# 8 of the 24 modulation units of the first attention layer move from TensorE to row products on VectorE, and the other 16 stand in a row behind units 31 to 46 of the hybrid block

## The reference, cut to what matters

```python
# first block: three branches from one wide product, gated and summed, then a feed forward
(hg_q, hg_f, hg_i, hg_g, ml_qk, ml_v, ml_if, ml_o, mb_z, mb_xbc, mb_dt, gate_pre) = split(rmsnorm(x) @ w_in)
x = x + (gates[0] * (y_hg @ w_br_hg) + gates[1] * (y_ml @ w_br_ml) + gates[2] * (y_mb @ w_br_mb)) @ w_out
u_g, u_v = split(causal_dwconv(rmsnorm(x) @ w_up))
x = x + (silu(u_g) * u_v) @ w_down
# two attention layers i = 0, 1
sh1, sc1, g1, sh2, sc2, g2       = split(silu(c)     @ w_ada[i] + b_ada[i], 6)    # w_ada[i] is 1024 x 6144
csh1, csc1, cg1, csh2, csc2, cg2 = split(silu(c_ctx) @ w_ada[i] + b_ada[i], 6)
h, hc = rms_norm(x) * (1 + sc1) + sh1, rms_norm(ctx) * (1 + csc1) + csh1
x = x + g1 * (mixed(h, hc) @ w_out[i])
x = x + g2 * conv_ffn(rms_norm(x) * (1 + sc2) + sh2)        # and the same for ctx in layer 0
```

## Time and profile before

| | |
|---|---|
| median of 3 runs | 1656.63 us (1656.02 to 1659.84) |
| span of the profiled execution | 1654.1 us |
| its own time | 1655.9 us |
| TensorE / VectorE / ScalarE / GpSimd busy | 97% / 74% / 53% / 11% |
| granted clock, mean | 0.995 |

### The profile page before, as it was taken

One profiled execution on the slowest core, in us unless ns is written; L12 is line 12 of the kernel. 1 busy time (PEld: TensorE's weight loads), 2 busy tenths in 40 slices (PEclk: granted clock), 3 DMA queues, 4 the chain that ended last, 5 costly groups with the idle time before them and its releaser, 6 DMA issues.

```text
span 1654.1 us, 34573 instructions
## 1 busy us (share of the span) xinstructions
PE 1596.3 (97%) x14802; PEld 1448.0 (88%) x14802; DVE 1215.8 (74%) x2069; ACT 881.4 (53%) x1344; POOL 189.4 (11%) x120
## 2 busy tenths in 40 slices
PE   8999999999999999999988999999999998799999
PEld 7999888898999999998867888888887897699999
DVE  4375499687877886588866788876888779568864
ACT  5435645548546665456775444323433456666653
POOL 4303540000000110100000011101110000041100
PEclk9999999999999999999999999999999999999999
DMA  7655555464455554531202243463435333045554
GB/s 280 249 215 227 195 219 183 169 230 179 145 187 179 184 191 158 182 109 54 76 2 74 107 153 128 146 232 142 155 136 207 110 103 103 3 157 200 202 167 143
DMA packets 41129, 259.67 MB, mean 157 GB/s; under 512 B 4368, under 2 KB 7696, under 8 KB 14480
## 3 DMA queue, kind: packets, MB, share of 16 engines
q1 hardware_dynamic: 40976, 257.46, 43.6%
HBM read 256.39 MB, written 1.05 MB: 156 GB/s over the span
## 4 chain that ended last, share of the span: by engine, by line
PE 68%; DVE 23%; ACT 4%; issue 2%; DMA 2%; DVEq 0%; SPq 0%; ACTq 0%
PE acc_psum L209 20%; PE acc_psum L210 19%; PE acc_psum L211 19%; DVE w_low_sb L174 5%; DVE mod_products L336 3%; DVE u_filtered L2116 2%; DVE ring_sb L336 2%; PE acc_psum L218 2%; DMA ring_sb<-in_w_up 1%; ACT w_high_sb L162 1%; PE acc_psum L2609 1%; DVE norm_rt_sb L1848 1%; PE acc_psum L272 1%; ACT norm_rt_sb L2869 1%; PE acc_psum L2638 1%
## 5 line engine op out<-in xcount | busy, mean ns | idle before, releaser
L209 PE MATMUL acc_psum<-h_high_sb,w_high_sb 128*128 128x256 f32 (+1 forms) x2176 | 655.8, 301 | 5.1 <-DVE h_low_sb L502 1.9
L210 PE MATMUL acc_psum<-h_low_sb,w_high_sb 128*128 128x256 f32 (+1 forms) x2176 | 647.9, 298 | 0.0
L211 PE MATMUL acc_psum<-h_high_sb,w_low_sb 128*128 128x256 f32 (+1 forms) x2176 | 647.9, 298 | 0.0
L162 ACT ACTIVATE w_high_sb<-ring_sb 128x1024 fp32r<-128x1024 f32 (+2 forms) x412 | 387.0, 989 | 359.3 <-PE acc_psum L211 212.5
L174 DVE TENSOR_TENSOR w_low_sb<-ring_sb,w_high_sb 128x1024 fp32r<-128x1024 f32 (+1 forms) x362 | 395.7, 1135 | 103.4 <-ACT w_high_sb L162 93.8
L209 PEld LDWEIGHTS acc_psum<-h_high_sb,w_high_sb 128*128 128x128 f32 x2176 | 411.1, 189 | 32.4 <-issue 12.7
L210 PEld LDWEIGHTS acc_psum<-h_low_sb,w_high_sb 128*128 128x128 f32 x2176 | 409.0, 188 | 15.5 <-issue 0.5
L211 PEld LDWEIGHTS acc_psum<-h_high_sb,w_low_sb 128*128 128x128 f32 x2176 | 408.8, 188 | 15.0
L2116 DVE SCALAR_TENSOR_TENSOR u_filtered<-acc_psum,par_sb,u_filtered 128x255 f32<-128x255 f32 (+2 forms) x264 | 150.7, 571 | 48.0 <-ACT u_filtered L2257 29.5
L2293 POOL TENSOR_TENSOR u_low<-u_filtered,u_high 128x256 fp32r<-128x256 f32 (+1 forms) x66 | 67.3, 1020 | 956.3 <-ACT u_high L2286 956.3
L209 PE MATMUL acc_psum<-u_high,w_high_sb 128*128 128x256 f32 (+1 forms) x539 | 169.7, 315 | 4.5 <-DVE w_low_sb L174 2.8
(11 more groups left out here) (310 smaller groups left out, 1875.4 us busy)
## 6 DMA issues: line engine op xcount, KB each, us to landing
ring_sb<-in_w_in SPq DMA_DIRECT2D x68, 1024.0 KB, 6.4
ring_sb<-in_w_up SPq DMA_DIRECT2D x66, 1024.0 KB, 4.9
ring_sb<-in_w_down SPq DMA_DIRECT2D x48, 704.0 KB, 4.2
ring_sb<-in_w_ada SPq DMA_DIRECT2D x24, 1024.0 KB, 4.8
ring_sb<-in_w_ada_rows SPq DMA_DIRECT2D x24, 1024.0 KB, 4.9
ring_sb<-in_w_out SPq DMA_DIRECT2D x12, 1024.0 KB, 4.8
ring_sb<-in_w_br_hg SPq DMA_DIRECT2D x4, 1024.0 KB, 6.9
ring_sb<-in_w_br_ml SPq DMA_DIRECT2D x4, 1024.0 KB, 4.8
```

Of the source, the lines that this page charges most:

```text
L162: self.nc.scalar.activation(self.high[:, self.shifted(c, g, piece)], self.ring[:, c % RING, piece], ACT.Copy)\
L209: nc.tensor.matmul(out, sh, mh, start=start, stop=False)
L210: nc.tensor.matmul(out, sh, ml, start=False, stop=False)
L211: return nc.tensor.matmul(out, sl, mh, start=False, stop=stop)
```

## The change

Of the 24 units of `w_ada[0]`, the first 16 ride behind units 31 to 46, one behind each, and are summed in one group of 16 (`TOGETHER`) with one copy and one reduction; `read` comes at n = 50. The last 8 are stored as rows and taken with `RowModulation.dot`: 4 in the hybrid block, in VectorE's iterations 2, 4, 6 and 8 (`EARLY_RIDES`), and 4 in the first down projection, behind units 2, 5, 8 and 11 of the stream, two instructions in one iteration and two in the next. The conditions' rows (1 MB) are fetched and passed through Silu on ScalarE twice for it: in the hybrid block at n == 2, and at n == 0 of the down projection. The low halves of units 0 to 7 go from GpSimd to VectorE, and unit 0's stands ahead of the first norm's reciprocal. In layer 1, the first pieces of `w_out_2` and of the last up projection move to VectorE as well.

```diff
-LOW_BY_POOL = ("q", "f", "ml_qk", "xbc")
+LOW_BY_POOL = ("ml_qk", "xbc")
-RIDES = tuple(range(1, 2 * (N_ADA * P // UNIT), 2))
-ROW_RIDES = {"out": (1, 2), "up0": (1, 3, 4, 6, 7, 9), ...
+RIDES = tuple(range(31,47))
+EARLY_ROWS = 8
+EARLY_RIDES = (3, 5, 7, 9)
+ROW_RIDES = {"first_up": (), "first_down": (2, 5, 8, 11), "out": (1, 2), "up0": (1, 3, 4, 6, 7, 9), ...
...
-    TOGETHER = 12
+    TOGETHER = 16
...
-    def dot(self, dve, n, c):
+    def dot(self, dve, n, c, tiles=(0, 1)):
...
         for s in range(2):
-            for j in range(2):
-                t, row = 2 * n + j, slot[:, j, :]
+            for j in tiles:
+                row, (bias, result) = slot[:, j, :], self.result(n, j)
...
-        ins.then_inc(*self.multiplied.one())
+        if 1 in tiles:
+            ins.then_inc(*self.multiplied.one())
...
+class EarlyRows(Hook):
+    def act(self, act, n):
+        if n == 0:
+            self.rows.activate(act)
...
-        add("w_down", range(2 * DT), "dve", "dve", NARROW)
+        add("w_down", range(2 * DT), "dve", "dve", NARROW, ROW_RIDES["first_down"])
...
+            core.split_low(dve, 0, "dve")
             norm1.reciprocal(dve)
...
+                if n + 1 in EARLY_RIDES:
+                    rows.dot(dve, EARLY_RIDES.index(n + 1), core.place(n + 1) + 1)
-                if n == 2 * NM + 2:
-                    mod.read(dve, NM // mod.TOGETHER)
+                if n == RIDES[-1] + 4:
+                    mod.read(dve, len(RIDES) // mod.TOGETHER)
...
+                for j in range(2) if both else ():
+                    if n + 1 - j in rides:
+                        side.dot(dve, m0 + rides.index(n + 1 - j), core.place(g0 + n + 1 - j) + 1, (j,))
```

More of the change, by code:

```diff
@@ L192, in release @@
             else:
-                self.sides += 1
-                sp.wait_ge(*side.multiplied.at(self.sides))
+                kind = self.stream[c][2]
+                self.sides[kind] += 1
+                sp.wait_ge(*{s.KIND: s for s in sides}[kind].multiplied.at(self.sides[kind]))
             self.load(sp, c + RING)
@@ L244 @@
 class Modulation:
+    KIND = "columns"
     GROUPS = 4
     RESULTS = UNIT
-    TOGETHER = 12
+    TOGETHER = 16
     ROWS = 2 * TOGETHER
@@ new lines, in hold, with fetch, activate, result @@
+    def hold(self, rows, products):
+        self.rows, self.products = rows, products
+        self.begun.append(self.taken)
+    def fetch(self, sp, src):
+        sp.dma_start(self.rows.rearrange("p a b -> p (a b)"), src).then_inc(*self.rows_in.dma())
+    def activate(self, act):
+        act.wait_ge(self.rows_in.handle, 16 * len(self.begun))
+        self.core.nc.scalar.activation(self.rows, self.rows, ACT.Silu).then_inc(*self.rows_ready.one())
+    def result(self, n, j):
+        (bias, result), t = (self.early, N_ADA - 2 * EARLY_ROWS + 2 * n + j) if n < EARLY_ROWS else (self.layer, 2 * (n - EARLY_ROWS) + j)
+        return bias[:, t, 0:1], lambda s: result[:, t, s:s + 1]
@@ L896, in build @@
             else:
-                add("w_up_2", range(up0, up0 + FFT), "dve", "pool", NARROW)
+                add("w_up_2", range(up0, up0 + FFT), "dve", "dve", NARROW)
                 add("w_down_2", range(down0, down0 + 2 * DT), "dve", "dve", NARROW)
-        assert counts == [NM, NM]
+        assert counts["columns"] == len(RIDES) and counts["rows"] == NM + EARLY_ROWS
         with nc.Block() as core.block:
@@ L1055, in hybrid_block @@
     mb = BranchNorm(core, 2, z, lambda t: pr("mb_norm", t), None, late_roots, 2, Y)
+    rows.hold(view(7 * W8, 2, D), rt[:, :].rearrange("p (a b) -> p a b", a=2))
+    rows.taken += len(EARLY_RIDES)
     x_ready = [sig(f"stream_ready_{half}") for half in range(2)]
@@ L2053, in _ @@
                 if side and n == 0:
-                    act.wait_ge(side.rows_in.handle, 16)
-                    core.nc.scalar.activation(side.rows[:, :, :], side.rows[:, :, :], ACT.Silu).then_inc(*side.rows_ready.one())
+                    side.activate(act)
                 if n >= 1:
@@ L2118, in feed_forward @@
         for p, first in enumerate(range(0, FFT, n)):
+            up_rides, down_rides = (ROW_RIDES[name] for name in (("first_up", "first_down") if seg == 1 else (f"up{p}", f"down{p}")))
             up(core, H, T, first, n, lambda ch: (cw(lead, ch), cb(ch)), conv3, tmp, uh, ul, None if p else norm,
-               up_banks, first_use, done_before, side, ROW_RIDES[f"up{p}"] if side else (), rest)
+               up_banks, first_use, done_before, side, up_rides if side else (), rest)
             free = core.sig("up_bank_free")
@@ L2393, in _ @@
                     core.split_low(dve, g0 + 1, "dve")
-                if n in rides:
+                if n in rides and not both:
                     side.dot(dve, m0 + rides.index(n), core.place(g0 + n) + 1)
```

101 lines of the change are left out of this document (59 added, 42 removed).

## The result

| | before | after |
|---|---|---|
| median | 1657.6 us (4 runs) | 1699.7 us (4 runs, 1697.8 to 1704.1) |
| span of the profiled execution | 1654.1 us | 1699.4 us |
| mean granted clock | 0.995 | 0.984 |

The change makes the kernel slower by 42 us: ratio 1.0253, 95% interval 1.0228 to 1.0277. The forecast had the sign and half the size, 1676.5 with a range to 1690.

The account below looks back on a forecast made before the run. TensorE's matmul queue (97% busy) bounds it, VectorE where TensorE waits. Terms −13.6 + 0.2 + 2.6 + 18.7 + 3 + 10.5 + 0.4 = +21.8 gave 1677.7, named 1676.5 us; range 1669 to 1685, wider 1659 to 1690.

Parts of the forecast that it names:

- The gain before unit 28: Units 1 to 25: 13 rides and one column reduce leave TensorE, −13.6 us, bounds −11 and −14.7.
- The ring's loop: Even units 34 to 40: weight load waits for the ride before it; 21.6 us per two units, +14.1 over three pairs.
- The down projection's +10.5: First down projection: Silu, late ring loads and dot products on VectorE lengthen it by 10.5 us, bounds +5 and +13.
- part (a): First down projection, unit 3: Silu of the rows precedes unit 2's copy on ScalarE and first dots wait, +2.2 us.
- Part (b): First down projection, units 5, 8, 11: loads issued only after the second pair of dots, three times 1.3, +3.9 us.
- The ride behind unit 27 goes as well: Behind unit 27: removing this ride gives nothing, since TensorE waits 1.8 us for VectorE there.
- about 1.3 of load waits: From unit 40 on: four added rides at 1.0 and these waits, less ride 47, +4.3 us.
- The clock, +3: Units 34 to 40: half clock after TensorE's waits, 1.35 us in two places and some in a third; bounds 0 and +5.
- The pitch: Rival, first up projection: matmul pitch 0.111 or 0.121 instead of 0.116, ±5 us; chance 0.1 either way, atop the others.
- the one on the other side: Rival, units 31 to 46: ring doesn't bind, loads are in time; 1647 to 1650 us, faster; chance 0.07.
- only one of the two delays is real: Rival: ring without down projection loss 1667 us, or down projection without ring and clock 1662 us; together 0.25.
- The rival of the clock that stays low: Rival: whole 48-matmul units run at 1.2 GHz after waits, up to 5 us in four to six places; 1690 to 1700; 0.08.

Follow-up runs that it names:

- fillers: The changed kernel plus 24, 20, 22 and 50 filler matmuls behind the rides of units 33, 35, 37 and 39: 1694.2 us, ratio 1.0232.
- resident_block: The changed kernel with its 16 rides multiplying a resident block of constants, their weights not loaded into the ring: 1671.9 us, ratio 1.0092.
- thin_loads: The changed kernel with each modulation unit's load cut to an eighth, slots, waits and matmuls kept: 1706.3 us, ratio 1.0296.

## Why the prediction was wrong

**What held.** The gain before unit 28 (−10.5 for −10.8), with the loss at units 6 and 7. The ring's loop, step by step, with 21.70 at full clock for a computed 21.6 (fillers, units 34 to 36). The down projection's +10.5, measured 11.4, in its three parts: unit 3 2.0 (2.2 forecast), units 4 to 11 4.3 (3.9), units 12 and 13 4.8 (4.4; the terms written there, 2 x 2.4 − 0.5, give 4.3). The reason given for part (a) was only half right: the products behind the Silu, not the Silu. Part (b) is in part luck: it laid 1.3 each on units 5, 8 and 11, and 1.7 came at unit 4, 0.3 at unit 5, 1.3 at unit 9 and 0.5 at unit 11.

**What failed.** The forecast's sum was +21.8, the profiled executions differ by 45.3 in span. Of the 23.5 between them 7.2 lie in point 1, 7.4 in point 2, 3.5 in point 3, 2.0 in point 4, and the rest in four small differences of some 1 us or less.

1. *"The ride behind unit 27 goes as well, ... so it gives nothing"*, and that the gain before it is kept. Between units 28 and 34 7.5 us went back, where the sum had 0.3. It asked what a removed ride gives, not what its absence makes earlier. 4.6 were lost up to unit 29, 4.0 of them GpSimd's subtraction on VectorE's gate sums (with unit 30's low half moved off GpSimd, 0.3 in place of 4.6). 1.3 net went in unit 29, where the half clock costs 2.5. The ride behind unit 29 goes too and stands nowhere in the sum; its 1.1 is what keeps this at 1.3. 1.8 were lost between units 32 and 34.
2. *Units 40 to 47, "about 1.3 of load waits"*. The term was +4.3 and measured +11.7. I held the loop for broken once the mLSTM heads were through, but each low half was still late, and the pieces behind it on VectorE (L1503, L1524) held up TensorE in their turn. resident_block shows 7.9 of ring there.
3. *The clock, +3*. Each of the three stretches paid 2.0 to 2.1, not two of them 1.35, about 6 in all; the region 34 to 40 measured +20.6 for 17.1. The 1.35 was also too low for its own rows, 4.4 − 2.76 = 1.64. The rule of the Trainium skill that was weighed (page "TensorE: Matmul & The Clock Gate", section "HAM oscillation — how this bites in real kernels"), that every such wait is paid anew, holds here for waits for VectorE, three times 0.50. I had priced it by the stretch in front of unit 34, of which only a part ran at half clock.
4. *The pitch.* In the profiled execution the up projection runs faster by 4.5 us and the last feed forward slower by 6.5. This was named as a rival within the range. It is no effect of the change that any run here shows: before_cut, the kernel before with its ten shortened rides, has both (−4.5 and +5.6), and thin_loads and the short products of the down projection don't have the gain. Net it is 2 of the 45.3.

The rivals: the ring did bind, so the one on the other side is out. That only one of the two delays is real is out as well; both are, the down projection at the price named and the ring with its clock at 32.3 for 21.4 between units 34 and 48, and more was missed between units 28 and 34. The pitch moved, as its rival had it, both ways within the range. The rival of the clock that stays low named 1690 to 1700, and the time fell there, but not by its mechanism: the clock was 1.00 again when units 36, 38 and 40 began, and each stretch paid 2 us, not up to 5. That is coincidence.

## What to carry to other kernels

Count ring slots in the order of the stream, and for each load name the one instruction that frees its slot: a second kind of entry behind every unit turned a prefetch of one unit into none, and thinning the traffic did nothing for it. A stretch with a constant period, whatever lies between, is such a loop; when it goes through a wait of several us on TensorE, add the half clock behind every wait. And before a gain on one engine is carried to the end, look at what it makes another engine do sooner, and beside what.

## What the runs showed of the hardware

These small operations of VectorE with two inputs in SBUF take six times as long beside a GpSimd subtraction (0.41 against 2.39 and 2.44 us on 4 and 16 partitions of 256), and a scan of 4x256 2.77 in place of 0.68. The two pieces of a low half take 5.73 in place of 2.36 (unit 30's in the variant that moved it to VectorE). Operations with one input in PSUM lose nothing: three of L1848 (128x255) take 1.52 beside GpSimd at 226.32 of the kernel before, and 1.51 without it at 237.66. The Trainium skill, page "GPSIMD Engine Reference", section "1. Specifications", says that GpSimd shares its SBUF interfaces with VectorE, with contention for instructions with two SBUF inputs. The rows agree, and add that small operations pay the most for their length: they seem to last about as long as one GpSimd subtraction does, 2.4 us, which no run here tests by itself.

The second thing is the pitch of matmuls. A long stretch of products runs at 0.113 or 0.118 us each nearly from start to end: the last feed forward, between the two marks in the table above, took 181.7 us in the kernel before and 188.2 in the changed one with the same matmuls, and 183.0 to 188.6 in the variants. Which of the two a stretch gets changed from kernel to kernel without a pattern I could find; it is 4 to 7 us of scatter that no edit here controls, and it stays open.
